# Two transformer blocks on one core: the first stage rebuilt (loads in another order on two queues, x through four banks, decay chain spread over heads)

## The reference

```
h = x * rsqrt(mean(x^2) + eps) * norm_mix_g            # 512 x 1024
q, k, v, xr, gr, g_attn, g_rnn = split(h @ w_in)       # q, k: 8 heads x 2 parts x 64; v: 8 x 128
q, k = rmsnorm(q, q_g), rmsnorm(k, k_g)                # over 64
p = softmax(q k^T / 8 + rel_bias[bucket(distance)], causal)   # two parts a head
attn = p[part 0] - lam * p[part 1];  out = rmsnorm(attn @ v, subln_g) * 0.2 -> w_proj_attn
log_a = -8 * sigmoid(..) * softplus(-lru_lambda)       # decay of the recurrence, used after head 7
```

## Time and profile before

| | us |
|---|---|
| median of 3 runs (2057.5 to 2059.64) | 2058.53 |
| profiled execution, its own time | 2057.48 |
| span of that execution | 2055.7 |
| TensorE busy | 1951.7 (95%) |
| VectorE busy | 1080.3 (53%) |
| ScalarE busy | 501.0 (24%) |
| GpSimd busy | 1237.3 (60%) |

### The profile page before, as it was taken

The page is one execution under the profiler, slowest core; times in us unless marked ns, Lnnn a source line. Parts: engine busy times, 40 slices in busy tenths (PEclk is TensorE's granted clock), DMA queues, the critical chain, the costliest instruction groups (busy, mean ns, idle before and its releaser), DMA issues.

```text
span 2055.7 us, 23472 instructions
## 1 busy us (share of the span) xinstructions
PE 1951.7 (95%) x9015; PEld 1598.3 (78%) x9015; DVE 1080.3 (53%) x1516; ACT 501.0 (24%) x1001; POOL 1237.3 (60%) x1018
## 2 busy tenths in 40 slices
PE   6888887999999999999999999999999899999997
PEld 4666666888888888888878777888778788888886
DVE  7666657999355231226876686333555473223134
ACT  4444443333122010112133333010222221001012
POOL 6233325788776776766633444676767567677662
PEclk8999998999999999999999999999999999999998
DMA  5122112333333333333322322333433233333321
GB/s 158 47 62 62 49 34 75 89 89 113 103 93 92 103 92 97 98 94 101 93 52 52 77 62 67 103 93 92 123 93 103 75 100 93 98 96 94 102 78 56
DMA packets 341169, 177.39 MB, mean 86 GB/s; under 512 B 14453, under 2 KB 338203, under 8 KB 341060
## 3 DMA queue, kind: packets, MB, share of 16 engines
q1 hardware_dynamic: 339044, 173.28, 29.3%
q10 hardware_dynamic: 2016, 2.62, 0.6%
HBM read 173.75 MB, written 2.13 MB: 86 GB/s over the span
## 4 chain that ended last, share of the span: by engine, by line
PE 74%; DVE 20%; ACT 3%; issue 3%; DMA 0%; ACTq 0%; SPq 0%; DVEq 0%
PE bank L649 21%; PE bank L653 21%; PE bank L651 21%; PE bank L767 2%; PE bank L744 1%; DVE aPR L1613 1%; PE bank L715 1%; DVE fPR L1878 1%; DVE aPR L1615 1%; DVE IT L1713 1%; DVE XC L1694 1%; DVE HS L1723 1%; DVE HS L1724 1%; DVE aPR L1605 1%; PE bank L733 1%
## 5 line engine op out<-in xcount | busy, mean ns | idle before, releaser
L618 POOL TENSOR_TENSOR WL<-RAW,WH 128x1024 fp32r<-128x1024 f32 (+3 forms) x331 | 813.1, 2457 | 27.7
L649 PE MATMUL bank<-HH,WH 128*128 128x512 f32 x1560 | 623.2, 399 | 9.3 <-DVE SQ L1573 7.4
L653 PE MATMUL bank<-HH,WL 128*128 128x512 f32 x1560 | 618.8, 397 | 0.0
L651 PE MATMUL bank<-HL,WH 128*128 128x512 f32 x1560 | 615.6, 395 | 0.0
L614 POOL TENSOR_TENSOR gate<-gate 128x1 f32<-128x1 f32 x331 | 86.6, 262 | 758.8 <-PE bank L653 710.3
L649 PEld LDWEIGHTS bank<-HH,WH 128*128 128x128 f32 x1560 | 296.0, 190 | 75.1 <-issue 16.8
L615 POOL TENSOR_SCALAR WH<-RAW 128x1024 fp32r<-128x1024 f32 (+3 forms) x331 | 342.8, 1036 | 0.9 <-issue 0.2
L653 PEld LDWEIGHTS bank<-HH,WL 128*128 128x128 f32 x1560 | 296.0, 190 | 60.4 <-issue 1.7
L651 PEld LDWEIGHTS bank<-HL,WH 128*128 128x128 f32 x1560 | 296.1, 190 | 60.2 <-issue 3.4
L1764 DVE TENSOR_TENSOR X<-X,bank 128x512 f32<-128x512 f32 x80 | 55.0, 687 | 200.6 <-PE bank L653 200.6
L1486 DVE SCALAR_TENSOR_TENSOR HL<-X,PARAM,HH 128x512 fp32r<-128x512 f32 x40 | 90.8, 2269 | 30.0 <-ACT HH L1091 30.0
(11 more groups left out here) (397 smaller groups left out, 3188.0 us busy)
## 6 DMA issues: line engine op xcount, KB each, us to landing
RAW<-in_w_in SPq DMA_DIRECT2D x107, 512.0 KB, 3.7
RAW<-in_w_up SPq DMA_DIRECT2D x32, 512.0 KB, 3.9
RAW<-in_w_down SPq DMA_DIRECT2D x32, 512.0 KB, 3.9
RAW<-in_w_ffn_gate SPq DMA_DIRECT2D x22, 512.0 KB, 3.6
RAW<-in_w_ffn_up SPq DMA_DIRECT2D x22, 512.0 KB, 3.7
RAW<-in_w_xkv SPq DMA_DIRECT2D x16, 512.0 KB, 3.8
RAW<-in_w_ffn_down SPq DMA_DIRECT2D x16, 512.0 KB, 3.5
RAW<-in_w_proj_attn SPq DMA_DIRECT2D x8, 512.0 KB, 3.9
```

The lines of the kernel that those rows point to most:

```text
L618: nc.gpsimd.tensor_tensor(WL[:, s, 0:k, :], RAW[:, s, 0:k, :], WH[:, s, 0:k, :].bitcast(F32), ALU.subtract).then_inc(S_[f"unit_cut{s}"], 1)
L649: mm(psum[s][:, 0:n], WH[:, s, k, :], hi(k), start=(k == 0), stop=False)
L651: mm(psum[s][:, 0:n], WH[:, s, k, :], lo(k), start=False, stop=False)
L653: last = mm(psum[s][:, 0:n], WL[:, s, k, :], hi(k), start=False, stop=(k == tiles - 1))
```

## The change

The order of the loads: SP issues the gain, x half 0, unit (0,0), x half 1, units (0,1), (0,2), the 16 row loads, and then the units of head 1, which before came after the bias rows. ScalarE's queue issues the one-hot rows, tables and lambdas.

x goes through four banks (`XBANK`). ScalarE makes `HH` straight from the bank, VectorE makes `HL` from the bank and `HH` and then copies the bank to `X`, for chunks 6, 4, 5, 7 later. The sums of squares are made per token: ScalarE squares `XTOK` (128x1024) with a running sum into `SSQ` (128x4), root and reciprocal are taken of 4 columns, ScalarE scales four identity blocks by them (`DIAG`), and a matmul with ones spreads that over the partitions. `RSTD` is a copy of that bank. TensorE interleaves the transposes of chunks 4 to 7 with the queries' products and starts the keys at the fourth chunk. Parameters, statistics and bias rows stand inside the values' products; 18 products of head 1 come before the first score, and head 0's share becomes (3, 10, 8, 3). The bias rows leave their banks on ScalarE. GpSimd clears the query tiles after its third split instead of before the first, and splits unit (1,1) only when the low parts of head 0's queries and keys are made. The decay chain becomes a generator, of which VectorE runs five steps in each head from 1 on.

The core of the diff:

```
+        XBANK = [WORK[0], WORK[1], psum[2], psum[3]]
+        X_LATE = (6, 4, 5, 7)
...
+            load_x(0)
+            load("qkv", 0, 0, cols(w["w_in"], 0))
+            load_x(1)
+            load("qkv", 0, 1, cols(w["w_in"], D))
+            load("qkv", 0, 2, cols(w["w_in"], D * 2))
...
             for j in range(3):
-                load("qkv", 0, j, cols(w["w_in"], D * j))
-            sp.dma_start(ONEHOT[:, 0:BIAS1_W], causal_rows).then_inc(S_["tab_landed"], 16)
...
+                load("qkv", 1, j, cols(w["w_in"], P + D * j))
             sp.wait_ge(*once("brow_rows"))
...
-            clear_queries("a", M1, M1["OR"][:])
...
+                if (name, it, j) == ("qkv", 1, 1):
+                    pool.wait_ge(S_["a_qk_lo"], 3)
                 cut(name, it, j)
+                if (name, it, j) == ("qkv", 0, 2):
+                    clear_queries("a", M1, M1["OR"][:])
...
+            queries0, keys0 = from_h("qkv", 0, 0, cut_of("n1")), from_h("qkv", 0, 1)
+            for e in range(DC):
+                run(queries0, 3)
+                if e < 4:
+                    x_transposed(e + 4)
+                if e >= 3:
+                    run(keys0, 3)
+            run(keys0)
+            pe.wait_ge(S_["n1_x"], 5)
+            values0 = from_h("qkv", 0, 2)
+            run(values0, 3)
+            parameters()
+            pe.wait_ge(S_["n1_diag"], NB)
+            mm(STAT[:], ones[:], DIAG[:], start=True, stop=True).then_inc(norm_event("n1", "stat", 0)[0], 1)
+            run(values0, 3)
+            bias_rows()
+            run(values0, 6)
             pe.wait_ge(*norm_event("n1", "std", 1))
...
+            steps0 = chain(*[from_h("qkv", 1, j) for j in range(3)])
+            run(steps0, 12)
...
+            run(steps0, 6)
...
+                if h == 0:
+                    steps, share = steps0, (3, 10, 8, 3)
...
+            def token_squares(t):
+                act.wait_ge(S_["n1_ssq"], t)
+                A(SQT[:], XTOK[:, t, :], ACT.Square, accum_out=SSQ[:, t:t + 1]).then_inc(S_["n1_ssq"], 1)
+            for e in range(DC):
+                act.wait_ge(S_["xt_done"], e + 1)
+                A(HH[:, e, :], XBANK[e % 4][:], ACT.Copy, scale=par(GAIN["n1"], e)
+                  ).then_inc(norm_event("n1", "hh", 0)[0], 1)
...
             for e in range(DC):
-                norm_chunk("n1", e, e % 2)
...
+                V.scalar_tensor_tensor(HL[:, e, :], XBANK[e % 4][:], par(GAIN["n1"], e), HH[:, e, :].bitcast(F32),
+                                       ALU.mult, ALU.subtract).then_inc(norm_event("n1", "hl", 0)[0], 1)
+                if e < 4:
+                    x_copy(e)
...
+            V.reciprocal(SSQ[:], SSQ[:]).then_inc(S_["n1_rstd"], 1)
...
+            V.tensor_copy(RSTD[:], STAT[:]).then_inc(norm_event("n1", "std", 0)[0], 1)
...
+                for _step in range(5 if 0 < h else 0):
+                    next(decays, None)
                 dve.wait_ge(S_["a_stat_read"], 3 * h + (3 if last else 5))
```

More of the change, by code:

```diff
@@ L375, in program @@
                 "n5": "ffn_norm_g_2", "n6": "final_norm_g_2"}
-        ACC, STD, SQS = ({tag: first if tag == "n1" else later for tag in GAIN}
-                         for first, later in ((ACC0, ACC1), (STD0, STD1), (SQ0, SQ1)))
+        ACC, STD, SQS = ({tag: tile for tag in GAIN if tag != "n1"} for tile in (ACC1, STD1, SQ1))
+        XBANK = [WORK[0], WORK[1], psum[2], psum[3]]
+        X_LATE = (6, 4, 5, 7)
         scr = nc.dram_tensor("bias_rows", [HEADS, BIAS1_W + BIAS2_W], F32).ap()
@@ L433, in _, with load_x @@
             sp.dma_start(VROWS[0:r, 0, :], w[name].rearrange("(r c) -> r c", c=P)).then_inc(S_["gain_landed"], 16)
-            for half in range(2):
+            def load_x(half):
                 sp.dma_start(XTOK[:, :, half * S:(half + 1) * S],
@@ L472, in _ @@
                 sp.dma_start(BIAS1[:, h, :], toeplitz_of(h, 0)).then_inc(S_[f"bias_landed{h}"], 16)
-            for h in range(1, HEADS):
+            for h in range(2, HEADS):
                 for j in range(3):
@@ L568, in _ @@
         def _(pool):
+            for s in range(SLOTS):
+                pool.sem_inc(S_[f"unit_cut{s}"], 1)
+                pool.sem_inc(S_[f"hi_made{s}"], 1)
             nc.gpsimd.memset(ident[:], 0.0).then_inc(once("ident_clear")[0], 1)
@@ L700, in _ @@
[L700 to L706, removed]
@@ L819, in head1 @@
+            mm(OUTB[:, 160:176], ones[0:1, :], SROW[0:1, 0:16], start=True, stop=True).then_inc(once("lam_done")[0], 1)
+            run(steps0, 6)
+            pe.wait_ge(*once("brow_rows"))
             def head1(h, last):
-                steps = chain(from_h("first", 0, 0), from_h("first", 0, 1)) if last else \
-                    chain(*[from_h("qkv", h + 1, j) for j in range(3)])
-                attend("a", M1, KIND1, h, steps, (2, 8, 8, 3) if last else (5, 10, 10, 2),
+                if h == 0:
+                    steps, share = steps0, (3, 10, 8, 3)
+                elif last:
+                    steps, share = chain(from_h("first", 0, 0), from_h("first", 0, 1)), (2, 8, 8, 3)
+                else:
+                    steps, share = chain(*[from_h("qkv", h + 1, j) for j in range(3)]), (5, 10, 10, 2)
+                attend("a", M1, KIND1, h, steps, share,
@@ L1139, in _ @@
+            act.wait_ge(S_["n1_ssq"], NB)
+            A(SSQ[:], SSQ[:], ACT.Sqrt, bias=EPSC[:], scale=1.0 / D).then_inc(S_["n1_root"], 1)
+            act.wait_ge(S_["n1_rstd"], 1)
+            for t in range(NB):
+                A(DIAG[:, t * P:(t + 1) * P], ident[:], ACT.Copy, scale=SSQ[:, t:t + 1]).then_inc(S_["n1_diag"], 1)
             act.preload_act_table_set("natural_log_exp_and_others")
@@ L1141, in _ @@
             A(LAMS[:, 2:4], LAMS[:, 0:2], ACT.Exp).then_inc(once("lam_exp")[0], 1)
-            act.wait_ge(*once("decay_abs"))
-            A(LOGT[:, 1, :], LOGT[:, 0, :], ACT.Exp, scale=-1.0).then_inc(once("decay_exp")[0], 1)
+            act.wait_ge(*once("brow_done"))
+            own.mark(A(BROW[:, 0:512], WORK[0][0:8, :], ACT.Copy))
+            A(BROW[:, 512:], WORK[1][0:8, :], ACT.Copy).then_inc(once("brow_rows")[0], 1)
+            own.wait()
             def load_bias1(h):
@@ L1563, in _ @@
+            dve.wait_ge(*once("par_done"))
+            own.mark(V.tensor_copy(PARAM[:, 8:80], OUTB[:, 8:80]))
+            own.link(V.tensor_copy(PARAM[:, 96:151], OUTB[:, 96:151]))
+            V.tensor_scalar(LOGT[:, 2, :], PARAM[:, column["lru_lambda"]:column["lru_lambda"] + 8],
+                            -1.0, None, ALU.mult).then_inc(once("par_taken")[0], 1)
             dve.wait_ge(S_["lam_landed"], 96)
```

197 lines of the change are left out of this document (103 added, 94 removed).

## The result

The changed kernel takes **2040.84 us** (median of 4 runs, 2037.31 to 2045.93), the kernel before in the same session 2058.02 (4 runs, 2055.91 to 2059.64): ratio 0.9919, 95% interval 0.9895 to 0.9943. Its profiled execution took 2041.82, 15.7 less than the 2057.48 of before.

The account below looks back on a forecast made before the run. TensorE, 95% busy, bounds the kernel, so only its idle or half-clock stretches can give time. From 2057.48, first score -13.6, head 0 -2.0 and decay +3.0 sum to -12.6: 2044.9, median 2046 us, range 2038 to 2053.5.

Parts of the forecast that it names:

- The first score: Start of head 0: first score at 44.0 against 57.58, -13.6 us, bounds 41.0 and 49.1.
- TensorE's own work: From first product to first score of head 0: matmuls and transposes sum to 28.1 us at full clock.
- Half clock: Between first product and first score: TensorE at half clock after idling adds 3.0 us, bounds 1.7 and 4.6.
- The wait for the squares of the queries: In head 0's values pass: TensorE waits about 1.0 us for squares behind two BROW copies on ScalarE.
- What keeps the products fed: Ahead of head 0's products: HL about 0.7 us each, squares 1.25 us each and hidden.
- C: Rival for the start: loads or HL don't improve, first score near 48, -8.6 us, 2050; chance 0.07.
- D: Rival for the start: 1.2 GHz up to the first score, at 69.1, total +12.5 us, 2071; chance 0.04.
- Head 0: From first score to head 0's end: less TensorE work saves at most 5.8 us, GpSimd's splits stall combines; -2.0 taken.
- rival A: Head 0 at about +1 as combines meet splits, decay steps +5: -7.6 us in all, 2051; chance 0.17.
- the forecast's bad end: In head 0: five combines stalled some 1.9 us more each (7.6), the 5.8 saving gone and some 2 lost.
- Decay steps: Tails of heads 1 to 5: linked steps wait for splits and delay aOR, +3.0 us, bounds 0 and 7.
- rival B: Better start, first score at 41.0 (-16.6), head 0 -3.5, decay +2: -18.1 us, 2040; chance 0.12.

Follow-up runs that it names:

- experiment 3: The changed kernel with SP's old order of loads, x in two halves and then all weights; one run, 2050.72 us.
- experiment 9: The changed kernel without the hold on GpSimd's split of unit (1,1) and with decay steps in VectorE's idle time inside the heads; 2032.45 us, ratio 0.9872.
- experiment 4: The changed kernel with HL made from X and HH, as before, instead of from the bank; one run, 2043.66 us.
- experiment 8: The changed kernel with each of ScalarE's four squares of 128x1024 made twice; one run, 2041.25 us.
- Experiment 1: The changed kernel without the wait that holds back GpSimd's split of unit (1,1); median 2040.55 us, ratio to before 0.992.
- Experiment 2: The changed kernel with the decay steps moved from behind aVR to between the two q/k normalisations; median 2037.06 us, ratio 0.9908.
- experiment 5: The kernel before with the decay spread alone, five steps in the tails of heads 1 to 5; ratio to before 1.0003.
- experiment 6: The changed kernel with all 24 decay steps ahead of head 0's q/k normalisation and decay_exp behind ScalarE's first two factors; one run, 2043.12 us.
- experiment 11: The changed kernel run once more, unaltered; 2040.20 us, ratio 0.9911.
- experiment 12: The kernel before run once more, unaltered; 2060.44 us.
- experiment 7: The changed kernel with the first weight issued ahead of both halves of x; one run, 2042.39 us.

## Why the prediction was right, and where its terms were off

**The first score: forecast 44.0, measured 42.81.** The mechanism is the one forecast, four of its terms were off, and they partly cancel. The first product came at 12.75, not 11.9, because the weight was usable at 9.06, not 8.1, and its split took 3.6, about as forecast: where the weight is loaded behind x's first half, the product followed the end of the split by 0.05 to 0.06 us in every profile. x was usable 1.0 later than taken, but that did not set the product. In eight profiles with this order of loads x came between 6.54 and 7.66; with the old order it came at 6.46 (experiment 3), and in three profiles of the old first stage at 6.22 to 6.32. For the one-hot rows, which experiment 3 has beside x too, the rule of the Trainium skill ("Trainium Kernel Development and Optimization", Key Constraints) had given an estimate of 0.3; the run shows 0.1 to 0.2, within what x moves from one profile to another. Where the prediction gives the first weight's late landing as what held the products of before, part of the reason is missing: behind the split, which ended at 16.81, TensorE had its transposes, parameters and bias rows to do until 20.76 (experiment 3). TensorE's own work was taken as 28.1; at full clock the stretch lasts 28.46 (experiment 9). Half clock was taken as 3.0 us and cost 1.6 (30.06 less 28.46, at a granted 0.94); the value of 1.7 named as the lower bound was right. The wait for the squares of the queries, taken as 1.0, was 0.2 (0.17, within the 28.46).

**What keeps the products fed: right.** HL at 0.74 to 0.75, squares at 1.06 and hidden (experiments 4 and 8). The normalisation was covered: there is no wait ahead of the score. Rivals C and D are out; the granted clock from 12.75 to 42.81 was 0.94.

**Head 0: forecast -2.0, measured -0.2.** This is the mis-sized term, and it is rival A's mechanism. The work did shrink, by 5.0 us. But the hold packs four splits over the softmax, TensorE's wait at the transposes grew from 1.58 to 4.78, and the clock fell to 0.86 of full behind that wait, where before it was 1.00. That second part, 2.2 us, was in no term. The eight large combines grew by 2.9 us (9.5 against 6.6), not by the 7.6 of the forecast's bad end. Experiment 1 shows 5.0 us to be due to the hold: without it head 0 was 5.3 shorter than before (29.7 against 35.0), near the 5.8 named as the most. So the step that failed is the middle taken between a saving and a stall, which left out what the stall does to the clock.

**Decay steps: forecast +3.0, measured +3.0** (heads 1 to 6 190.9 us against 187.9; 0.65 to 0.73 in each of four, 0.3 in the last; the third step blocked for 2.2 us). Experiment 2 takes nearly all of them off again. That the spread is worth having at all is not shown: alone it moved nothing (experiment 5), and experiment 6, with 1.3 us for it in one profile, carries a wait of its own.

**What was not in the sum.** The median is 5.2 us below the forecast of 2046, under the forecast's own 2042 and next to rival B's 2040, but not for B's reasons: the first score came 1.8 later than B has it, and head 0 and the decay gave none of B's extra. The marks up to head 6 add to -14.8 - 0.2 + 3.0 = -12.0, against -12.6. That they agree so closely is in part luck: the first score was 1.2 better than forecast and head 0 1.8 worse. Head 7 brought 3.6 more: it ran at 0.94 instead of 0.83. No instruction of it is changed; over all profiles with the new first stage it took from 26.1 to 30.4 us, and in experiment 5, with the old first stage, it took 27.0. So these 3.6 us can't be credited to the change on this evidence. They make up the difference between the -12.0 and the -15.7 of the two profiled executions; the medians differ by 17.2, and no profile shows where the last 1.5 lie. In the second pair of profiles (experiments 11 and 12) the first score is 15.6 earlier, the end of head 6 13.0 and the span 20.3. Whether the new stage makes half clock rarer later on, or whether it was chance, stays open. The two medians of the changed kernel, 2040.8 and 2040.2, suggest that it is not all chance, but no run here moves the later stretches in time and leaves the rest as it is.

## What to carry to other kernels

Price a stall of the engine that bounds the kernel by its length and by the clock behind it: here 2.8 us of delay cost 5.0 by the end of the head, though the saving showed in the time only with the decay steps moved too (experiment 9). Before small linked instructions are moved, see what GpSimd does at that place: an operation on 128x8 elements took 0.17 us beside an idle GpSimd and 2.20 inside a subtraction, so look for a gap without a split before you cut steps. Don't judge a gain of a few microseconds by one execution's total: compare marks, then repeat the runs.

## What the runs showed of the hardware

- Seven heads between 2 and 5 (experiments 1, 3, 5, 8 and 11) were 1.1 to 1.3 us longer than the same head of the changed kernel; all seven had a granted clock of 0.95 where the others had 1.00. Which head is hit differs from kernel to kernel, and between two profiled executions of the changed kernel.
- The record of the clock can miss it. In experiment 11 it shows 1.00 from 12.41 on, but two products that follow each other start 0.43 us apart; in experiment 2 the same two are 0.23 apart:

```profile
13.00 0.63 PE L652 MATMUL bank<-HL,WH 128*128 128x512 f32 x1
13.43 0.63 PE L654 MATMUL bank<-HH,WL 128*128 128x512 f32 x1
```

```profile
12.47 0.39 PE L652 MATMUL bank<-HL,WH 128*128 128x512 f32 x1
12.70 0.40 PE L654 MATMUL bank<-HH,WL 128*128 128x512 f32 x1
```

  From the first product to the first score, experiments 3, 7, 8 and 11 took 29.6 to 30.3 us at a recorded 1.00, where experiments 2 and 9 took 28.5.

- The same first loads in the same order let x be used between 6.54 and 7.66 us and the first weight between 8.05 and 9.28, in eight profiles of seven kernels, and the first product followed between 11.75 and 12.98.
